# Position biases laid out backwards by a constant table and read backwards by GpSimd

## The reference, cut to what matters

```
bucket = t5_causal_bucket(n)          # n < 16: n itself; then logarithmic; 31 from about n = 113 on
logits = q . c / 8 + rel_bias[bucket]  # 8 heads, 32 buckets
out    = softmax(logits over the selected keys) . c
```

## Time and profile before

| | |
|---|---|
| median of 3 runs | 1232.89 us (1232.23 to 1233.17) |
| profiled execution, its own time | 1233.68 us |
| its span, first to last instruction | 1231.9 us |
| PE matmul busy | 1186.3 us (96%), 5525 instructions |
| DVE busy | 846.7 us (69%) |
| ACT busy | 545.5 us (44%) |
| POOL busy | 522.3 us (42%), 420 instructions |
| DMA moved | 118.62 MB, mean 96 GB/s |

### The profile page before, as it was taken

One profiled execution on the slowest core, in us unless ns is written; L12 is line 12 of the kernel. 1 busy time (PEld: TensorE's weight loads), 2 busy tenths in 40 slices (PEclk: granted clock), 3 DMA queues, 4 the chain that ended last, 5 costly groups with the idle time before them and its releaser, 6 DMA issues.

```text
span 1231.9 us, 16224 instructions
## 1 busy us (share of the span) xinstructions
PE 1186.3 (96%) x5525; PEld 954.2 (77%) x5525; DVE 846.7 (69%) x1275; ACT 545.5 (44%) x891; POOL 522.3 (42%) x420
## 2 busy tenths in 40 slices
PE   4999999889999999999999999989999999999997
PEld 3786687568788778788788779878888888888886
DVE  6378987777867888888988878868533343333357
ACT  4535643775175244243244276652442433433440
POOL 2134695765446776776775653221002103003002
PEclk9999899999999999999999999999999999999999
DMA  7731532002314233242243200044223433333331
GB/s 224 241 94 47 193 94 78 1 1 103 103 52 133 89 112 111 86 136 88 86 132 102 82 21 1 1 155 120 88 100 88 118 88 101 105 100 86 120 103 68
DMA packets 126852, 118.62 MB, mean 96 GB/s; under 512 B 5773, under 2 KB 99530, under 8 KB 126794
## 3 DMA queue, kind: packets, MB, share of 16 engines
q1 hardware_dynamic: 126794, 117.86, 31.3%
HBM read 107.34 MB, written 10.50 MB: 96 GB/s over the span
## 4 chain that ended last, share of the span: by engine, by line
PE 85%; DVE 5%; POOL 5%; issue 2%; ACT 2%; DMA 1%; POOLq 0%; DVEq 0%; ACTq 0%
PE g_bank L1681 16%; PE g_bank L1682 15%; PE g_bank L1683 15%; PE wide L1681 9%; PE wide L1683 9%; PE wide L1682 9%; PE g_bank L1843 3%; PE g_bank L1646 2%; POOL wlo L460 2%; PE wide L1801 1%; PE wide L1745 1%; PE wide L1746 1%; POOL rows L874 1%; DVE logit L1076 1%; DVE probs_lo L1089 1%
## 5 line engine op out<-in xcount | busy, mean ns | idle before, releaser
L460 POOL TENSOR_TENSOR wlo<-wring,whi 128x1024 fp32r<-128x1024 f32 (+1 forms) x94 | 229.7, 2445 | 194.9 <-ACT whi L1552 117.0
L1681 PE MATMUL g_bank<-xhi,whi 128*128 128x512 f32 (+2 forms) x768 | 301.2, 392 | 2.1 <-DVE xlo L701 1.6
L1682 PE MATMUL g_bank<-xlo,whi 128*128 128x512 f32 (+2 forms) x768 | 297.5, 387 | 0.0
L1683 PE MATMUL g_bank<-xhi,wlo 128*128 128x512 f32 (+2 forms) x768 | 297.5, 387 | 0.0
L1552 ACT ACTIVATE whi<-wring 128x1024 fp32r<-128x1024 f32 x120 | 127.1, 1059 | 356.2 <-PE wide L1683 179.8
L460 DVE TENSOR_TENSOR wlo<-wring,whi 128x1024 fp32r<-128x1024 f32 (+1 forms) x66 | 84.4, 1279 | 199.1 <-ACT whi L1552 192.7
L1681 PE MATMUL wide<-whi,hhi 128*128 128x512 f32 x480 | 190.2, 396 | 0.8 <-POOL wlo L460 0.8
L1682 PE MATMUL wide<-wlo,hhi 128*128 128x512 f32 x480 | 189.6, 395 | 0.0
L1683 PE MATMUL wide<-whi,hlo 128*128 128x512 f32 x480 | 189.6, 395 | 0.0
L1681 PEld LDWEIGHTS g_bank<-xhi,whi 128*128 128x128 f32 (+1 forms) x768 | 144.2, 188 | 39.1 <-issue 6.2
L1682 PEld LDWEIGHTS g_bank<-xlo,whi 128*128 128x128 f32 (+1 forms) x768 | 144.2, 188 | 33.1 <-issue 2.1
(11 more groups left out here) (248 smaller groups left out, 1923.8 us busy)
## 6 DMA issues: line engine op xcount, KB each, us to landing
wring<-in_w_up SPq DMA_DIRECT2D x64, 512.0 KB, 4.1
wring<-in_w_down SPq DMA_DIRECT2D x64, 512.0 KB, 3.7
wring<-in_w_in SPq DMA_DIRECT2D x26, 512.0 KB, 3.8
wring<-in_w_o SPq DMA_DIRECT2D x16, 512.0 KB, 4.6
rows<-in_x SPq DMA_DIRECT2D x8, 512.0 KB, 5.2
normalized_rows<-rows SPq DMA_DIRECT2D x8, 512.0 KB, 6.8
rows<-normalized_rows SPq DMA_DIRECT2D x4, 512.0 KB, 5.1
emb_stage<-normalized_rows SPq DMA_DIRECT2D x4, 512.0 KB, 4.6
```

The lines of the kernel that those rows point to most:

```text
L460: eng.tensor_tensor(parts_of(name, lo_tile(name)), parts_of(name, wring[n % 4]), parts_of(name, hi_tile(name)).bitcast(F32), ALU.subtract) ...
L1681: nc.tensor.matmul(out_ap, w_hi, m_hi, start=first, stop=False)
L1682: nc.tensor.matmul(out_ap, w_hi, m_lo, start=False, stop=False)
L1683: return nc.tensor.matmul(out_ap, w_lo, m_hi, start=False, stop=last)
```

## The change

The constant table is handed over reversed along its 384 columns, so that the row in DRAM is reversed. It is then loaded from its second element on, straight into `near_bias`, with the same shift by one element per partition. So `near_bias[p, h, j]` is the old row at 382 - p - j, and the masks read it from element `near - 1` down to 0. `near_up`, `flip`, the four products, the four copies, the PSUM uses `near` and SP's wait for `wuv_lo_ready` are gone (four uses fewer leave every later bank as it was); POOL waits for `bias_in` once in each of the two calls of `head_masks`.

```diff
@@ bucket_differences
-    return hot
+    return np.ascontiguousarray(hot[:, ::-1])
@@ psum_uses
-    names += [("near", n) for n in range(4)] + [("ql", 0, h) for h in range(HEADS)]
+    names += [("ql", 0, h) for h in range(HEADS)]
@@ tiles
-        near_up = part("near_up", 32, [P, HEADS, NEAR])
-        flip = sb("flip", [P, P])
@@ SP
             sp.wait_ge(bias_out, 16)
-            sp.wait_ge(wuv_lo_ready, 1)
-            sp.dma_start(near_up[:, :, :], bass.AP(tensor=bias_rows.tensor, offset=0, ap=[[1, P], [FWIN, HEADS], [1, NEAR]])
+            sp.dma_start(near_bias[:, :, :], bass.AP(tensor=bias_rows.tensor, offset=1, ap=[[1, P], [FWIN, HEADS], [1, NEAR]])
@@ POOL, start
-            pool.memset(flip[:, :], 0.0).then_inc(const_steps, 1)
-            pool.wait_ge(const_steps, 2)
-            pool.affine_select(out=flip[:, :], in_=flip[:, :], compare_op=ALU.not_equal, fill=1.0, base=1 - P,
-                               pattern=[[1, P]], channel_multiplier=1).then_inc(ident_ready, 1)
-            pool.wait_ge(const_steps, 6)
+            pool.wait_ge(const_steps, 5)
@@ POOL, head_masks
                 pool.wait_ge(g_full, EV[LAST_UNIT])
+                pool.wait_ge(bias_in, 16)
-                                       near_bias[:, h, NEAR - near:NEAR], ALU.add).then_inc(mask_full, 1)
+                                       near_bias[:, h, near - 1::-1], ALU.add).then_inc(mask_full, 1)
@@ ACT
             products(0)
-            for n in range(4):
-                copy_out(("near", n), near_bias[:, 2 * n:2 * n + 2, :],
-                         bank(("near", n))[:, :].rearrange("p (h n) -> p h n", h=2))
-
             act.wait_ge(score_added, 16)
@@ PE
-            pe.wait_ge(ident_ready, 2)
+            pe.wait_ge(ident_ready, 1)
             products(0)
-            pe.wait_ge(bias_in, 16)
-            for n in range(4):
-                free(("near", n))
-                nc.tensor.matmul(bank(("near", n))[:, :], flip[:, :], near_up[:, 2 * n:2 * n + 2, :].rearrange("p h n -> p (h n)"),
-                                 start=True, stop=True).then_inc(g_full, 1)
             latent_queries(0)
```

## The result

The changed kernel takes **1236.67 us** (median of 20 runs, 1232.16 to 1239.95), the kernel before 1232.63 (20 runs, 1231.13 to 1237.31). The ratio is 1.0029, with a 95% interval from 1.0020 to 1.0039: slower by 0.29%. The forecast of 1232.5 was wrong, and so was its range, which ended at 1235.4. Its profiled execution took 1238.26 us, with a span of 1236.5.

A forecast was written before the change was run, and what follows sets the result against it. PE bounds the kernel (85% of the chain of waits); the removed products' 1.67 us head start is nearly all lost waiting for DVE. Sum -0.30 - 0.10 + 0 = -0.4 us, median 1232.89 to 1232.5 us; range 1231.0 to 1235.4.

The forecast's parts named there:

- The clock doesn't change this: PE's 1.2 GHz stretch, 128.0 to 134.4 us, may come earlier or last longer; 1.5 us lost only eats PE's wait.
- The clock rival: PE's longer wait before 190 us draws the lower clock afterwards: 3.2 - 0.4 = +2.8 us, 1235.7; chance 0.03.
- Head start: Without the products and copies, PE runs 1.67 us ahead from the latent queries to its next meeting with DVE.
- Absorbed at PE's wait for L1098: Chunk 1's value product: PE arrives at 188.31, waits some 2 us for DVE; nearly all of the 1.67 us goes.
- DVE's gain: DVE's list beside POOL: L1036 0.30 us sooner, L1098 0.1 us; 0.4 us gain, from -0.4 to 1.67.
- The reading as such: DVE's L1036, 1.21 us for 384 elements: held until POOL's operation ends, then 0.22 us of work.
- the losing case: L1036 on DVE: with POOL ahead by only 1 us, DVE falls on the start of L722 and loses 0.4 us.
- Backward read: POOL's masks reading with a negative step: taken to cost nothing, wide mask staying at 0.73 us.
- Both rivals that hung on this read: POOL's masks: backward operand fetched at half speed, 1234.7, chance 0.15; backward read doubling the mask, 1241.2, chance 0.12.
- Edits at nothing: POOL's fill and select for `flip`, `ident_ready` count, SP's wait, the load and POOL's wait for `bias_in`: no cost or gain.

The follow-up runs named there:

- 2: Changed kernel, with two superfluous products of constants on PE before the first value product of chunk 1, filling its wait; 1232.55 us, ratio 0.9997.
- 6: Kernel before, with one superfluous DVE operation between its selection and the latents, making PE's wait longer; 1235.99 us, ratio 1.0020.
- 10: Kernel before, with PE's waits at the ends of both attentions filled with products of constants; 1232.06 us, ratio 0.9992.
- 11: Changed kernel, with PE's wait near 188 us and its waits at the ends of both attentions filled; 1232.41 us, ratio 0.9996.
- 3: Changed kernel, with four unused products and copies put back where the old ones stood, direct load and backward read kept; 1232.49 us, ratio 1.0005.
- 4: Changed kernel, with projection u1 of chunk 1 put ahead of the first value product; 1231.62 us, ratio 0.9988.
- 5: Changed kernel run again, unchanged; 1236.71 us, ratio 1.0029.
- 1: Kernel before run again, unchanged; 1232.86 us (12 runs), ratio 0.9999.
- 12: Kernel before, with u1 ahead of the first value product and fills at the attention ends and before input transposes; 1229.58 us, ratio 0.9968.
- 8: Changed kernel, with u1 ahead of the first value product and fills at the attention ends and before input transposes; 1228.08 us, ratio 0.9966.
- 9: Changed kernel, with PE's waits at the ends of both attentions filled, the wait near 188 us left; 1232.93 us, ratio 0.9996.

## Why the prediction was wrong

**The step that failed** is "The clock doesn't change this", with its last sentence: "Even 1.5 us lost by it would only eat PE's 2 us of waiting at 188 us." It looked for the low clock ahead of the wait. The low clock came behind the wait, where no slack is left: 1.54 us in the trace, shown by taking the idle time away (2), and by making it alone (6). The clock rival named this place and mechanism, and the low stretch that the earlier trace rows showed was the evidence for it. I priced it at half of 6.4 us, +2.8 in all and 1235.7, and gave it 0.03. Its total is short by only 1 us, but that is luck: at its one place 1.54 us were lost for 3.2 priced, and it didn't know of the other two, which cost 2.61 and 1.48 in the profile. The half of the clock step that looked ahead of the wait was right: 0.48 us of the head start were lost there and went out of the wait.

**Head start: right.** 1.70 us at 124 us after 1.67, of which 1.22 reached the wait. **Absorbed at PE's wait for L1098: right.** DVE ended a tenth before PE went on, 2.21 us of waiting after "some 2". Experiments 10 and 11 are level once the clock is out at the three places.

**DVE's gain: wrong, and small.** L1036 was to lose 0.30 us. It took 1.33 at 156.96, 0.12 more than in the earlier trace rows, since it fell just behind the start of L719; L1092, which was L1098, took 1.21 after 1.22. The reading as such (held until POOL's operation ends, then 0.22 us of work) was right in 13 of 14 profiles. From the sixteenth score to the end of the latents DVE needed 73.07 us after 72.79: +0.28 for a forecast -0.4. The forecast moved POOL's operation forward by 1.67 us against DVE, into 0.6 us before it. POOL came forward by 2.92 (159.71 to 156.79) and DVE by 1.68 (158.64 to 156.96), so by 1.24: between that and the losing case that the forecast named ("were POOL ahead by only 1 us"), and 0.17 us before DVE. The 0.4 us by which this differs from the forecast come from the 0.48 that PE lost in the low stretch at 125: here too the clock was the term left out.

**Backward read: right at nothing.** 733 after 734 ns, and experiment 3 at 1.0005. The rule of the Trainium skill (GPSIMD Engine Reference, "Performance pitfalls for Q7 kernels") on steps above 8 bytes, taken by the size of the step as the sum took it, leaves a step of -4 bytes without a surcharge, and the trace agrees; taken by the unsigned value it would give about 1.1 us, which is refuted. Both rivals that hung on this read, 0.15 and 0.12, are refuted too. The first had an error in its sum: 2.2 less 1.8 us of lead leaves 0.4 and not 0.8, so its price was 1234.3 and not 1234.7.

**Edits at nothing: right.** The first two masks stand in the chain for 1.09 and 1.11 us, and the first `rstd` of POOL and the first transpose of PE begin at 6.24 and 9.23 us, the second again by the arrival of a DMA.

**What stays open.** The low stretches at 272 and 818 us cost 2.61 and 1.48 us in the profile of the changed kernel, more than the one at 190. PE's waits ahead of them are the same in both kernels: 1.41 and 1.69 us between 269 and 273, and 2.49 us at 813 (before) and 816 (after). All four profiles without the products and with the ends unfilled (after, 2, 4 and 5) have both stretches; of four with the products (before, 1, 3 and 6) only 6 has one, at 817. Yet in the timed executions of experiment 2 the clock was mostly as high as before. Why these waits meet 1.2 GHz so much more often behind a low stretch at 190 is not settled. Where a stretch begins against the work differs between executions of one kernel, so the four and four may differ by that alone; eight profiles are few for this, and it wasn't tried further. Nor is the stretch at 22 us tied to the change: 10 and 12, which have the products, lack it.

## What to carry to other kernels

Where PE is the bound and an edit turns its work into waiting, price the wait twice: the time that it absorbs, and the 1.2 GHz that may follow it, where there is no slack. Look for a stretch of clock 0.50 behind thin work in the profile of before, and take it as a warning for the next wait, but not as its price: the stretch there was of 6.8 us, the one behind the wait of 3.4. Then move real work into the wait, or fill it with products that compute nothing, before judging the edit: here the same removal was +4 us by itself and -1.5 us with the waits filled (8 against 12, on two chips).

## What was not expected of the hardware

A wait of 2.2 us in otherwise dense work was followed by 3.4 us at 1.2 GHz; waits of 0.7 us in the same place were not, in the five profiles that have one (before, 1, 3, 9 and 10). The length of a wait alone doesn't decide it: PE's wait of 2.49 us near 813 us had no low stretch behind it in the profiles of before, 1 and 3, and had one in after, 2, 4, 5 and 6. The fills and the new order of experiment 8 together moved the kernel before by 3.4 us and the changed one by 8.6, more than any of the edits to its real work. And the medians hide groups of executions, which the mean clock of each helps to tell apart: 24 of the changed kernel's 32 stand at 0.991 or below, against 11 of 99 of the kernel before.
